# A two-block transformer kernel: memory keys and values projected beside the last attention, and x as the first input

## The reference

```python
# first block, first step
u = rmsnorm(h, norm_mix_g[l])            # h is x itself
proj = u @ w_in[l]                       # 2048 x 8720

# second block, between its mixers and its MLP
x = x + jnp.concatenate([a, bb], axis=-1) @ w_out[l]
hc = rmsnorm_2(x, g_cross[l])
mem_n = rmsnorm_2(mem, g_mem[l])
x = x + memory_cross_attention(hc, mem_n, w_q_cross[l], w_k_cross[l], w_v_cross[l], w_o_cross[l])

def memory_cross_attention(h, mem_n, wq, wk, wv, wo):
    b, s, _ = h.shape
    m = mem_n.shape[1]                                   # 256
    q = (h @ wq).reshape(b, s, X_HEADS, X_HEAD_DIM)      # 4 heads of 128
    k = (mem_n @ wk).reshape(b, m, X_HEADS, X_HEAD_DIM)
    v = (mem_n @ wv).reshape(b, m, X_HEADS, X_HEAD_DIM)
    sc = jnp.einsum('bshd,bmhd->bhsm', q, k).astype(jnp.float32) * (X_HEAD_DIM ** -0.5)
    p = jax.nn.softmax(sc, axis=-1).astype(v.dtype)
    o = jnp.einsum('bhsm,bmhd->bshd', p, v).reshape(b, s, X_HEADS * X_HEAD_DIM)
    return o @ wo
```

## Time and profile before

| | us |
|---|---|
| median of 3 runs (2589.67 to 2590.25) | 2590.18 |
| the profiled execution's own time | 2588.82 |
| its span | 2586.9 |
| PE busy in it | 2555.4 |
| DVE busy, ACT busy | 1408.9, 1190.0 |
| mean granted clock of TensorE | 0.998 |

### The profile page before, as it was taken

The page is one execution under the profiler, slowest core; times in us unless marked ns, Lnnn a source line. Parts: engine busy times, 40 slices in busy tenths (PEclk is TensorE's granted clock), DMA queues, the critical chain, the costliest instruction groups (busy, mean ns, idle before and its releaser), DMA issues.

```text
span 2586.9 us, 32313 instructions
## 1 busy us (share of the span) xinstructions
PE 2555.4 (99%) x12005; PEld 2144.4 (83%) x12005; DVE 1408.9 (54%) x1609; ACT 1190.0 (46%) x1570; POOL 178.6 (7%) x184
## 2 busy tenths in 40 slices
PE   8999999999999999999999999999999999999998
PEld 6888888888888888888888988888788888888887
DVE  6465545465554444454555677566655445544554
ACT  6455544444544443444445455445544334443443
POOL 3000111011100000000001130101200000000000
PEclk9999999999999999999999999999999999999999
DMA  8754546667666666666655654646465666656654
GB/s 273 236 170 126 178 146 184 192 186 242 213 192 187 189 186 193 191 193 187 189 183 179 184 177 130 181 140 213 135 203 179 192 193 192 184 183 195 188 185 155
DMA packets 249253, 480.21 MB, mean 186 GB/s; under 512 B 15088, under 2 KB 33696, under 8 KB 247984
## 3 DMA queue, kind: packets, MB, share of 16 engines
q1 hardware_dynamic: 246304, 464.40, 59.2%
q0 software_dynamic: 2800, 14.23, 1.5%
q10 hardware_dynamic: 32, 0.01, 0.0%
HBM read 475.40 MB, written 3.17 MB: 185 GB/s over the span
## 4 chain that ended last, share of the span: by engine, by line
PE 96%; DVE 1%; ACT 1%; issue 1%; POOL 0%; DMA 0%; ACTq 0%; SPq 0%; POOLq 0%; DVEq 0%
PE acc L1262 90%; PE unit L1285 3%; PE psO L1416 1%; PE psS L1344 0%; PE psS L1388 0%; DVE w_lo L1534 0%; PE unit L1344 0%; ACT w_hi L1033 0%; POOL rtmp L892 0%; DMA mem_sb<-in_mem 0%; DVE gla L1781 0%; PE unit L1467 0%; POOL stat L880 0%; ACT p L1157 0%; DVE xT_lo L1539 0%
## 5 line engine op out<-in xcount | busy, mean ns | idle before, releaser
L1534 DVE TENSOR_TENSOR w_lo<-w_raw,w_hi 128x1024 fp32r<-128x1024 f32 (+4 forms) x892 | 1080.5, 1215 | 1012.4 <-ACT w_hi L1033 1007.5
L1033 ACT ACTIVATE w_hi<-w_raw 128x1024 fp32r<-128x1024 f32 (+4 forms) x892 | 925.1, 1041 | 1041.4 <-PE acc L1262 1025.0
L1262 PE MATMUL acc<-w_hi,xT_hi 128*128 128x512 f32 (+4 forms) x2432 | 943.8, 388 | 3.5 <-DVE w_lo L1534 3.5
L1262 PE MATMUL acc<-w_lo,xT_hi 128*128 128x512 f32 (+4 forms) x2432 | 933.0, 384 | 0.0
L1262 PE MATMUL acc<-w_hi,xT_lo 128*128 128x512 f32 (+4 forms) x2432 | 932.1, 383 | 0.0
L1262 PEld LDWEIGHTS acc<-w_hi,xT_hi 128*128 128x128 f32 x2432 | 457.2, 188 | 88.4 <-DVE w_lo L1534 4.2
L1262 PEld LDWEIGHTS acc<-w_lo,xT_hi 128*128 128x128 f32 x2432 | 456.8, 188 | 86.3
L1262 PEld LDWEIGHTS acc<-w_hi,xT_lo 128*128 128x128 f32 x2432 | 457.4, 188 | 82.8 <-issue 0.5
L1262 PE MATMUL acc<-w_hi,hT_hi 128*128 128x512 f32 x864 | 337.0, 390 | 0.0
L1262 PE MATMUL acc<-w_lo,hT_hi 128*128 128x512 f32 x864 | 336.2, 389 | 0.0
L1262 PE MATMUL acc<-w_hi,hT_lo 128*128 128x512 f32 x864 | 336.1, 389 | 0.0
(11 more groups left out here) (312 smaller groups left out, 1422.2 us busy)
## 6 DMA issues: line engine op xcount, KB each, us to landing
w_raw<-in_w_in SPq DMA_DIRECT2D x168, 512.0 KB, 3.6
w_raw<-in_w_up SPq DMA_DIRECT2D x128, 512.0 KB, 3.8
w_raw<-in_w_down SPq DMA_DIRECT2D x128, 512.0 KB, 3.7
w_raw<-in_w_ffn_gate SPq DMA_DIRECT2D x88, 512.0 KB, 3.8
w_raw<-in_w_ffn_up SPq DMA_DIRECT2D x88, 512.0 KB, 3.7
w_raw<-in_w_ffn_down SPq DMA_DIRECT2D x88, 512.0 KB, 3.7
w_raw<-in_w_out SPq DMA_DIRECT2D x64, 512.0 KB, 4.1
w_raw<-in_w_in SPq DMA_DIRECT2D x24, 368.0 KB, 3.6
```

Source lines behind the costliest of these rows:

```text
L1033: act.activation(w_hi[:, slot, 0:kc, 0:n], w_raw[:, slot, 0:kc, 0:n], ACT.Copy).then_inc(hi_split, 1)
L1262: ins = pe.matmul(ac[t][:, 0:n], a[:, l0 + c, t * P:(t + 1) * P], w[:, slot, c, 0:n], start=start and c == 0 and m == 0, stop=stop and c = ...
L1534: dve.tensor_tensor(w_lo[:, slot, 0:kc, 0:n], w_raw[:, slot, 0:kc, 0:n], w_hi[:, slot, 0:kc, 0:n].bitcast(F32), ALU.subtract).then_inc(lo_ ...
```

## The change

The list begins with x. It is loaded in the eight pieces that `mem` had before, and transposed by the kind "gain", so POOL's product and the buffer for it are gone. The first tile of `w_in` is cut by token half: its six matmuls for t = 0 come first, then the six for t = 1, then the transposes of the next columns, then two leads. `bias_row` stands behind the third tile of the second block.

`mem` is loaded during the second half of `w_out_2`, once PE has made the last transpose of the sparse attention (`load_mem`), and its eight transposes stand behind tiles 7 to 14 of that half, ahead of those of u where both follow one tile. The keys are projected next, then the queries, then the values with the steps of the cross attention behind their tiles. All four `output` steps follow the values, into `psO` and `psS` in turn; `pT` has four slots. Keys and values stay in SBUF.

```diff
-    mem_dense = block_steps("w_k_cross_2", 0, DC, 0, 512, "memT", 0, "ckv", 0, ("mem0", "mem1", "mem2", "mem3"))
-    mem_dense += block_steps("w_v_cross_2", 0, DC, 0, 512, "memT", 0, "ckv", 1)
...
-    S += [("keep_ckv",), ("bias_row",), ("half_rms",)]
...
+    first = w(0, 512, "qkva", 0, ("x0", "x1", "x2", "x3"))
+    S += [("gain_T", "x"), T(0, 0), ("lead",), T(0, 1), ("lead",)]
+    S += [("part", first[0][1], 0, 0), ("part", first[0][1], 0, 1), T(1, 0), T(1, 1), ("lead",), ("lead",)]
+    S += weave(first[1:], [[T(2, 0), ("gain_T", "mem")], [T(2, 1)], [T(3, 0)] + ssq(1, 0), [T(3, 1)] + ssq(1, 1),
+                           ssq(1, 2), ssq(1, 3) + roots(1)], 1)
+    S += [("half_rms",)]
+    S += weave(w(512, 512, "qkva", 512), [[], [], [("bias_row",)]], 1) + w(1024, 512, "qkva", 1024)
...
+    steps = into_norm(5, [make_block("w_out_2", 8, 8, 512 * j, 512, "xT", 8, "add", 512 * j, () if j else ("s0", "s1"))
+                          for j in range(4)], {(2, 1): 0, (2, 3): 1, (3, 2): 2})
+    turned = [[("T", f"mem{j}", t)] for j in range(4) for t in range(NT)]
+    S += weave(steps, [[], [], [("load_mem", 0)], [("load_mem", 1)], [("load_mem", 2)], [("load_mem", 3)], []] + turned, 1)
+    k = block_steps("w_k_cross_2", 0, DC, 0, 512, "memT", 0, "ckv", 0, ("mem0", "mem1", "mem2", "mem3"))
+    S += weave(k, [roots(5), both("u3"), ssq(0, 0), ssq(0, 1), ssq(0, 2), ssq(0, 3) + roots(0)], 1)
+    S += weave(block_steps("w_q_cross_2", 0, DC, 0, 512, "xT", 0, "cqo", 0, U_NEEDS), [[], both("ck"), [("gain", 6)]], 1)
     g = GROUP0["C"]
...
+    S += weave(block_steps("w_v_cross_2", 0, DC, 0, 512, "memT", 0, "ckv", 1),
+               [[("T", "cqq", 0)], [("T", "cqq", 1)], [("scores", g)], [("scores", g + 1)], [("probs_T", g), ("scores", g + 2)],
+                [("probs_T", g + 1), ("scores", g + 3)], [("probs_T", g + 2)]], 1)
+    S += [("probs_T", g + 3), ("output", g), ("output", g + 1), ("output", g + 2), ("T", "co", 0), ("lead",), ("output", g + 3)]
     o = make_block("w_o_cross_2", 0, 4, 0, 512, "coT", 0, "add", 0, ("co",))
-    S += [("part", o, 0, 0), ("output", g + 3), ("part", o, 1, 0), ("T", "co", 1), ("part", o, 0, 1), ("part", o, 1, 1)]
-    S += [("lead",), ("lead",), ("evac", o, (0, 1))] + pieces_of_norm(6, 0)
+    S += [("part", o, 0, 0), ("T", "co", 1), ("part", o, 1, 0), ("lead",), ("part", o, 0, 1), ("part", o, 1, 1)]
+    S += [("evac", o, (0, 1))] + pieces_of_norm(6, 0)
...
+                elif s[0] == "load_mem":
+                    j = s[1]
+                    c = slice(512 * j, 512 * j + 512)
+                    sp.wait_ge(unit_done, LAST_UNIT["s1", 1] + 1)
+                    sp.dma_start(mem_sb[:, :, c], tok(t_in["mem_2"][0])[:, :, c]).then_inc(mem_in[j], 16)
...
+                    if kind == "C":
+                        pe.wait_ge(out_done, max(GROUP0["C"], g - 1))
+                        pe.wait_ge(sc_read, GROUP0["C"] + NGROUPS["C"])
+                        if g == GROUP0["C"]:
+                            for tt in range(NT):
+                                block_read(pe, BLOCK["ckv", 1], tt)
+                    elif g:
                         pe.wait_ge(out_done, g)
```

More of the change, by code:

```diff
@@ L591, in build @@
         ang = arena("ang", [P, 4, NT, 32], 100)
+        mem_sb = arena("mem_sb", [P, NT, D], 80)
+        memT = (arena("memT_hi", [P, DC, SEQ], 23, F32R), arena("memT_lo", [P, DC, SEQ], 39, F32R))
         ckv = arena("ckv", [P, 2, NT, 512], 0)
@@ L747, in attention, with slot, out_bank @@
             scale = {"M": (M_NOPE + M_ROPE) ** -0.5, "S": S_DIM ** -0.5, "C": C_DIM ** -0.5}[kind]
-            return s2, p2, pT2, scale, 128
+            return s2, p2, pT4 if kind == "C" else pT2, scale, 128
+        def slot(kind, g):
+            return g % (4 if kind == "C" else 2)
+        def out_bank(kind, g):
+            return psS if kind == "C" and g % 2 else psO
         def values(kind, kt, h):
@@ L1026, in _ @@
         def _(act):
-            act.dma_start(gain_rows[:], t_in["g_mem_2"][0].rearrange("(c p) -> c p", p=P)).then_inc(gain_mem_in, 16)
+            for which, vec in (("x", "norm_mix_g"), ("mem", "g_mem_2")):
+                act.dma_start(gain_rows[which][:], t_in[vec][0].rearrange("(c p) -> c p", p=P)).then_inc(gain_rows_in[which], 16)
             def split_hi(i, slot, uses, free, kc=CK, n=COLS):
@@ L1063, in _ @@
                 elif s[0] == "gain_T":
-                    act.wait_ge(gain_turned, 1)
-                    act.activation(gain_T[:], psO[:, 0, 0:DC], ACT.Copy).then_inc(gain_T_ready, 1)
+                    act.wait_ge(gain_turned, 1 + (s[1] == "mem"))
+                    act.activation(gain_T[s[1]][:], psO[:, s[1] == "mem", 0:DC], ACT.Copy).then_inc(gain_T_ready[s[1]], 1)
                 elif s[0] == "ssq":
@@ L1112, in _ @@
                         acc_ready(act, b, 0, last)
-                        norm_known(act, 0, 1)
-                        act.activation(ckv1[:, arg, 0, :], ac[0][:], ACT.Copy, scale=over_rms(0, 0)).then_inc(
+                        norm_known(act, 0, at["root"])
+                        act.activation(ckv[:, arg, 0, :], ac[0][:], ACT.Copy, scale=over_rms(0, 0)).then_inc(
                             acc_free[b % 2][0], 1)
                     elif what in BUF and 0 in s[2]:
-                        if what == "gla" and arg == 0:
-                            act.wait_ge(gained, 8)
                         acc_ready(act, b, 0, last)
@@ L1360, in _ @@
                     pe.wait_ge(ident_in, 16)
-                    pe.wait_ge(gain_mem_in, 16)
-                    pe.transpose(psO[:, 0, 0:DC], gain_rows[:], ident[0:DC, 0:DC]).then_inc(gain_turned, 1)
+                    pe.wait_ge(gain_rows_in[s[1]], 16)
+                    pe.transpose(psO[:, s[1] == "mem", 0:DC], gain_rows[s[1]][:], ident[0:DC, 0:DC]).then_inc(gain_turned, 1)
                 elif s[0] == "T":
@@ L1415, in _ @@
                         for kt in range(nk // P):
-                            ins = pe.matmul(psO[:, i, 0:dv], pT[:, g % 2, i * (nk // P) + kt, :], values(kind, kt, range(NHEADS[kind])[two_heads(kind, h)][i]),
+                            ins = pe.matmul(out_bank(kind, g)[:, i, 0:dv], pT[:, slot(kind, g), i * (nk // P) + kt, :], values(kind, kt, range(NHEADS[kind])[two_heads(kind, h)][i]),
                                             start=kt == 0, stop=kt == nk // P - 1)
```

122 lines of the change are left out of this document (43 added, 79 removed).

## The result

The changed kernel takes 2619.1 us (median of 4 runs, 2617.8 to 2622.5) against 2590.2 for the kernel before on the same chip: 1.0114 times as long, 95% interval 1.0102 to 1.0126. I had forecast 2595 and a range of 2590.5 to 2599.5. It is slower by 28.9 us, not by 5. The profiled execution took 2617.93, span 2616.1.

What follows compares the result with a forecast made beforehand. PE's matmuls were taken to bound the kernel, so only its waits could change. Terms -0.5 - 1.1 + 0.15 + 7.7 - 1.0 = +5.25 gave 2595.4 us on the median, forecast as 2595, range 2590.5 to 2599.5.

Steps and rivals of the forecast that it cites:

- It can only win or lose where PE waits: Whole kernel: matmuls set the time and their number stays, but for one tiny transpose, so only PE's waits can change.
- the middle of the kernel keeps its banks and slots: Middle of the kernel: units, blocks and tiles removed at the front are even in number, so banks and slots stay.
- its transpose (0.15): The second gain vector's transpose: adds under 0.3 us, taken as +0.15.
- upper bound of +9.5: Second half of w_out_2: largest loss allowed, said to add tile 9's excess (1.4) once more to 7.7.
- Start, -0.5: Kernel start: first six matmuls need only the first transpose and go up to 1.9 us earlier; 0.5 us gain taken.
- End of the first transposes, -1.1: End of x's transposes: bias_row's 1.1 us wait goes, as it now stands behind a tile with a free bank.
- Second half of w_out_2, +7.7: Mem's transposes ahead of u's pairs: three share two banks; waits of 3.5 us at tile 9, 4.2 at 11 and 14.
- Cross attention, -1.0: Cross attention: old waits of about 5.6 us go, new ones of 4.6 come; between -5.6 and +1.
- The ring's turn: Cross attention: one turn of exp, w_hi, w_lo, scale, maximum on ACT and DVE takes 4.67 us, against PE's 4.07.
- The clock: Rival, chance 0.05: PE's clock falls at tile 9 behind 3.5 us of waits, costing 1.8 us: 2597.
- Late weight tiles: Rival, chance 0.12, second half of w_out_2: mem's 2 MB delay weight tiles; 3 us over would give 2598.5.
- Outcome by sign: Whole kernel: chances of slower by over 0.2% about 0.46, within 0.2% about 0.50, faster 0.04.

Runs made afterwards that it cites:

- turns_moved: Also called experiment 9: changed kernel with gain_T_mem in unused room, arena back in place, and mem's transposes at tiles no pair of u follows; 2588.94 us, ratio 0.9999.
- before_all64: Kernel before with every SBUF tensor 64 bytes higher, so distances between them stay as they were; 2589.78 us, ratio 1.0000.
- experiment 1: Changed kernel with one line edited: gain_T_mem lies in room another tensor leaves unused, so x_sb and the arena lie where they did before; 2597.15 us, ratio 1.0030.
- experiment 5: Kernel before with the three weight-tile rings 64 bytes higher, xT and constants 128 higher, x_sb and the arena unmoved; 2635.63 us, ratio 1.0176.

## Why the prediction was wrong

- **The step that failed** is "It can only win or lose where PE waits": that an equal number of matmuls takes an equal time, at the places that the change leaves alone above all ("the middle of the kernel keeps its banks and slots"). It put the time of all dense products outside the waits at nothing. I asked what moved in order and in time, and did not ask what moved in memory. The spacing of xT, in w_out_2 too, did stay at 0.2268; that of hT and yT, in stages where nothing changed, rose by 3% and cost 19.5. The diff shows `gain_T_mem` put ahead of `X0`; I priced its transpose (0.15) and not its place. The missing term is +22: 2619.1 - 2597.15 in the changed kernel, 20.2 in the kernel before.
- **The rest of the sum** was near: without that term 2597.15, and 2595.4 forecast on the median. The range would have held it, in part by luck: three falls of the clock that the sum did not have add 4.8, and the kernel before has one of 1.5 that the changed one does not.
- *A slip in a bound.* The upper bound of +9.5 for the second half of w_out_2 does not follow from its own terms, 7.7 + 1.4 = 9.1.
- *Start, -0.5.* The third tile began at 19.64 against 19.83, -0.2; x's first piece landed 0.6 later in that execution (first transpose at 5.25 against 4.66). In turns_moved's trace, with that transpose at 4.65, the third tile began at 19.18, so -0.65. This place is no steadier than that in one kernel: before_all64, the kernel before in all but addresses, began it at 20.81. The third tile's w_lo was late as described, by 0.91.
- *End of the first transposes, -1.1.* Right: the product of relb follows a tile without idle time, where it waited 0.97.
- *Second half of w_out_2, +7.7.* Right in place and mechanism, 7.0 in size: 3.0 at tile 9 and 2.02 at tiles 11 and 14. Experiment 9 shows the cause.
- *Cross attention, -1.0.* The ring's turn was 4.66 (exp at 1834.51, 1839.17) against my 4.67, the first output waited 2.7 against 2.9, and the product of coT 0.5. The outputs at the low level, 1.6, were not in the sum.
- *The clock*, a rival with a chance of 0.05, was no rival but came on top, at three places: twice in w_out_2 and once in the cross attention, about 1.6 each (priced at 1.8). Before each stands a wait of 2.0 to 3.0 with only transposes in it or beside it. The rule of the Trainium skill (TensorE: Matmul & The Clock Gate, Part 4: PE-mode transpose), that transposes do not count as the other matmuls do, agrees with the trace at these places. But the wait of 2.02 at tile 11, with the same transposes around it, had no fall behind it, and the one near 390 in the kernel before came without a transpose. So the rows do not say when one comes, and its cause stays open. The sum for experiment 1: 2595.4 forecast, - 0.7 (waits of 7.0 for 7.7), + 1.6 + 1.6 + 1.6 (low level), - 1.5 (the low-level stretch of the kernel before near 390) = 2598.0, against 2597.15 measured and 2596.6 to 2598.9 in its seven executions.
- *Late weight tiles.* Late, but under cover as reckoned: ACT waited for four tiles of w_out_2 from 1709.6 on, 3.2 us at most, and PE for no w_lo there.
- *Outcome by sign.* I gave slower 0.46 and no change 0.50. Without the shift the change measures 0.3% slower.

## What to carry to other kernels

A new buffer is an edit of every address behind it. Before pricing an edit, compare the addresses of all matmul operands, not only the order of instructions, and put small late additions into holes or at the end. When PE's busy time grows with an equal number of instructions, read the groups by shape and compare one operand's rows with another's: what got slower names the memory that moved. In this kernel the only distance of the stationary operand from the weight tiles that was free, of those tried, is a multiple of 256 bytes. Before dividing a stretch of the trace by its count, ask for the groups inside it: a stretch can hold two operands, of which one has changed. And a wait of 2 to 3 us of PE can cost 1.6 more by the clock behind it; in the changed kernel's trace, after the start, it did so at three of five such waits.

## What the runs showed of the hardware

- The spacing of back-to-back 128x128 by 128x512 products in fp32r depends on how far the stationary operand lies in SBUF from the rings of weight tiles modulo 256: for hT 0.2268 us at 0, 0.2335 at +32 and +64, 0.2326 at 128, 0.2291 at -64 (twice); for xT 0.2333 at +64. That is up to 3%, in a kernel of about 10,000 such products 46 us (experiment 5). Of the distances tried only 0 modulo 256 was free of it. A stretch of 192 narrower products, mostly of 416 columns, was not slowed at +64 (35.23 against 35.40). Why the distance counts, no run shows.
- The same wait of PE (2.54 to 2.56 for one w_lo in the first block) is followed by 12 products in 4.52 in the kernel before and in 3.04 in the changed one. The granted clock right behind the wait was 0.50 in the first, the lower level, and 1.00 in the second.
- The Trainium skill (TensorE: Matmul & The Clock Gate, Step-by-step: what each phase is for) says that PE has two independent read ports to SBUF, and that loading the next weights takes no read bandwidth from the running matmul. The mean length of hT's weight loads was 188 ns before and 187 in the changed kernel, which fits that. But by experiments 4 and 5 the pace depends on where the stationary operand lies to the weight tiles, so it is not the same wherever the two lie. Whether it is the reads by PE or the work of DMA, ACT and DVE in the rings beside them that costs the time was not tried.
